# Two-layer decoder trunk: modulation in 512-column tiles, first pair's chunks ahead of the last values, output transposes with a bank of their own

## The chip, the cores and the metric

One NeuronCore of one Trainium2 chip runs the whole program. The metric is the device time of one execution in microseconds (us); lower is better. TensorE is called PE, VectorE DVE, ScalarE ACT, GpSimd POOL and SyncE SP.

## What is computed

A trunk of two decoder layers over 512 tokens of width 1024, in float32, conditioned by a vector c. Each sub-layer is RMSNorm, then a shift and a scale that come from c, then the mixer or the FFN, then RMSNorm, a gate, and the residual add:

```python
def ada_mod(c_act, w, b, n):
    m = c_act @ w + b
    return jnp.split(m[:, None, :], n, axis=-1)
...
        shift, scale, gate = ada_mod(c_act, mod_mix_w[l], mod_mix_b[l], 3)
...
        h = rms_norm(x, norm_pre_mix[l]) * (1.0 + scale) + shift
        if l < N_A_LAYERS:
            y = dilated_mixer(h, a_w_qkv[l], a_w_o[l], cos, sin)
...
        x = x + gate * rms_norm(y, norm_post_mix[l])
```

Layer A's mixer has three groups of 8 heads of 64 (window and dilation 128/1, 512/4, 2048/16), each with its own q, k and v from `a_w_qkv`; the groups' outputs are merged by softmax over their log-denominators. Layer B is differential attention with 8 heads. Both FFNs are gated convolutions of 2816 features. Almost all the arithmetic is the products with the weights.

## The kernel before, in words

**Numbers.** A float32 operand is split into a head `hi` (rounded to the PE's fp32r form, written by ACT) and a rest `lo = full - hi` (DVE), and a product is three PE products: hi·hi, hi·lo, lo·hi. Weights come in chunks of 128 x 1024 by SP's queue into `raw` (three buffers, L404 to L431), are split into `whi` (ACT, L965) and `wlo` (DVE, L1374), and are used by 24 PE products of 512 columns. Chunk n+3 is loaded when chunk n's rest is done.

**Order.** There is no planner: each engine has its own stream, written out by hand, with counting semaphores. `tjob` is a stream of small PE jobs (transposes, one-column products) that share two PSUM banks in turn (`job`, L516): a job waits until the job two before it has been read.

**The start (L652 to L727 on PE, L1079 to L1131 on ACT, L1576 to L1617 on DVE).** SP loads x (2 MB), then eight tiles `mstart` of the first modulation matrix, 1024 rows by 256 columns each, two and then a chunk of value weights in turn (L434). Of a pair of tiles, the shift's 256 columns are made on PE alone (`shift_columns`, L674: 16 one-column products, 32 instructions), the scale's by a chain of eight multiply-adds on DVE (`scale_sums`, L1576) and two column sums over partitions on PE (`scale_columns`, L684). Both Sine operations of the rope tables and the four scalings of x are ACT's (L1085 to L1092). PE turns x in eight jobs of four tiles (L719), ACT copies each to `z0` (L1097). Then, for each of four pairs of feature tiles, ACT writes gain·z + shift twice (full and head, L1107, L1108), DVE the rest (L1611), and PE runs the values chunk of that pair (`values_chunk`, L701). The next pair's shift and scale jobs stand ahead of each values chunk on PE (L722).

**Layer A's attention.** PE then runs the values of groups 1 and 2 (eight chunks), and the six q/k chunks of the first pair of heads (`first_pair`, L750). Each q/k chunk is rotated by DVE (`rope`, L1626, four operations), headed by ACT (L1158) and rested by DVE (L1645, L1647). `attend_pair` (L761) handles a pair of heads in four classes of positions. With `proj` it runs the next pair's six chunks between its own steps. The last turn has none: per pass p it makes the scores of p+1, transposes of the finished output of pair p (`turn_o`, L807, two-bank jobs too; ACT reads the head at L1149, DVE the rest at L1707), transposes of the probabilities, and the products with the values (L804). Warming products (`keep_warm`, L508) fill in. DVE finds maxima (L1694) and sums one half of later modulation per mod_half (L1480), four multiply-adds of 256 columns.

**The token stages.** `token_stage` (L607) multiplies the mixer's output with its out matrix and adds the gated norm. It waits until the last output is transposed and read, runs the first chunk's two token tiles (12 products), spreads the gains over the partitions (`spread_gain`, L542, from diagonals made by DVE at L1387), waits until ACT has read them (L977), and goes on.

Of the kernel before, what the change touches and what calls it, by code (L numbers as in the profile page):

```python
# [114 lines left out]
def yoco_trunk(nc, x, c, positions, mod_mix_w, mod_mix_b, mod_ffn_w, mod_ffn_b,  # L115
# [16 lines left out]
    WARM = 24  # L132
# [10 lines left out]
    with ExitStack() as ctx:  # L143
# [174 lines left out]
        qk_rests = signal("qk_rests", "gsplit")  # L318
        table_natural = signal("table_natural", "table_natural")
# [49 lines left out]
        x_scaled = signal("x_scaled", "x_scaled")  # L369
        m_known = signal("m_known", "m_known")  # L370
# [8 lines left out]
        V_HALVES = (0, 0, 1, 1, 1, 1, 1, 2, 1, 1, 1, 2)  # L379
# [21 lines left out]
        def _(sp):  # L401
# [32 lines left out]
            for n in range(DT // 2):  # L434
                for j in (n, n + DT // 2):
                    sp.dma_start(mstart[:, j], columns(mod_mix_w[0], 2 * P * j, 2 * P)).then_inc(mods_landed[j].sems[0], 16)
                load_values(0, n)
# [3 lines left out]
            for pair in range(PAIRS):  # L441
                for g, w in KINDS:
                    load(columns(a_w_qkv[0][:, (g * 3 + w) * A_INNER:(g * 3 + w + 1) * A_INNER], pair * P))
# [35 lines left out]
        def _(pe):  # L479
# [127 lines left out]
            def token_stage(hi, lo, kt, diags=None, gated=False, norms=True):  # L607
# [6 lines left out]
                pe.wait_ge(*at.done(t_free, -2))  # L614
                pe.wait_ge(*at.done(t_free, -1))
                for b in range(3):
                    pe.wait_ge(*at.done(acc_free, -1 - b))
                for k in range(kt - 3):
                    operands(k)
                    for t in range(NT):  # L620
                        if k == 0 and t == 2 and diags is not None:

                            for diag in diags:
                                spread_gain(diag)
                            pe.wait_ge(*at.done(t_free, -2))
                            pe.wait_ge(*at.done(t_free, -1))
# [47 lines left out]
            def shift_columns(j):  # L674

                bank = job()
                pe.wait_ge(*at.done(mods_landed[j]))
                for half in range(2):
                    for k in range(DT):
                        ins = pe.matmul(bank[:, half:half + 1], mstart[:, j, k, tile_cols(half)], csil[:, k:k + 1],  # L680
                                        start=(k == 0), stop=(k == DT - 1))
                job_done(ins)

            def scale_columns(j):  # L684

                pe.wait_ge(*at.done(m0_summed, j))
                columns_of([macc0[:, 2 * j + half, :] for half in range(2)])

            def values_chunk(g, c):
# [5 lines left out]
                for t in range(NT):  # L695
                    if g and c == 0:
                        pe.wait_ge(*at.done(v_out, t - NT))
                    for k in (2 * c, 2 * c + 1):
# [22 lines left out]
            scale_columns(0)  # L721
            for c in range(DT // 2):  # L722
                if c < DT // 2 - 1:
                    shift_columns(c + 1)
                    scale_columns(c + 1)
                values_chunk(0, c)
            at.passed("h", DT)  # L727
            for g in (1, 2):
                for c in range(DT // 2):
                    values_chunk(g, c)  # L730
                    if (g, c) in ((1, 2), (2, 2)):
                        pair_columns(2 * g - 2, 2)
# [17 lines left out]
            def first_pair():  # L750

                for s in range(6):
# [4 lines left out]
                    if s == 1:  # L757
                        pair_columns(4, 2)
                pe.wait_ge(*at.done(v_out, -1))

            def attend_pair(proj, pair):  # L761
# [45 lines left out]
                def turn_o(n):  # L807

                    turn_tiles([oA[:, n, t, :] for t in range(NT)])
# [40 lines left out]
                if not proj:  # L850
                    keep_warm(2, ps[:, 0, :])
                    pe.wait_ge(*at.done(o_out, -1))
                    turn_o(PAIRS - 1)

            first_pair()
# [1211 lines left out]
```

## Time and profile before

| | us |
|---|---|
| median of 3 runs | 1525.46 |
| lowest, highest | 1522.84, 1529.31 |
| the profiled execution | 1524.3 |
| its span | 1522.5 |
| mean granted PE clock | 0.963 |

The span is that of one profiled execution; the 1.8 us beside it lie around the program. The page splits the span into 40 slices of 38.06 us, and gives for each the busy share of an engine in tenths and the PE clock that was granted, in tenths of full speed (0.5 is 1.2 GHz). DMA moves 313 GB/s in the first slice and 113 on average.

### The profile page before, as it was taken

To read this page: it belongs to the slowest core of one execution; us is meant where nothing else is said; L and a number is where in the kernel's file an instruction comes from. 1 tells how busy PE (TensorE), PEld (TensorE's weight loads), DVE (VectorE), ACT (ScalarE), POOL (GpSimd) and SP (SyncE) were. 2 spreads that over 40 slices of the span, in tenths; PEclk is the share of its full clock that TensorE was granted. 3 is DMA by queue.
4 is the path that set the end of the run, shared out by engine and by line. 5 is a ranking of instruction groups with operands and counts; after the bars stand their busy time and mean duration, and the time that the engine had idled before them with its cause. 6 is when DMAs were issued, how large, how long until landed. Compare 5 with 4: busy or idle time off the path is not lost.

```text
span 1522.5 us, 18985 instructions
## 1 busy us (share of the span) xinstructions
PE 1444.0 (95%) x7234; PEld 1188.0 (78%) x7243; DVE 886.9 (58%) x1540; ACT 584.0 (38%) x1003; POOL 136.5 (9%) x218
## 2 busy tenths in 40 slices
PE   6999899997899999999999999888799999999998
PEld 5888788886788878887887877676579888887886
DVE  5557687684168777763556675766256644443223
ACT  6333343443353334332115454455243333333112
POOL 1010001000021111110113000010021000000000
PEclk9799999896999999999999999999799999999999
DMA  9364334230026655553652212111015433333231
GB/s 313 124 195 145 95 109 126 83 111 14 15 77 200 199 174 178 182 179 97 199 174 61 61 56 59 55 55 56 28 56 153 138 97 97 97 97 90 91 96 69
DMA packets 176787, 171.40 MB, mean 113 GB/s; under 512 B 5205, under 2 KB 153030, under 8 KB 176710
## 3 DMA queue, kind: packets, MB, share of 16 engines
q1 hardware_dynamic: 162352, 119.59, 26.2%
q0 software_dynamic: 13824, 50.34, 10.2%
q8 instruction: 52, 0.85, 0.2%
q10 hardware_dynamic: 534, 0.41, 0.1%
q14 instruction: 25, 0.20, 0.0%
HBM read 168.22 MB, written 2.10 MB: 112 GB/s over the span
## 4 chain that ended last, share of the span: by engine, by line
PE 80%; issue 12%; DVE 5%; POOL 1%; ACT 1%; DMA 0%; SPq 0%; POOLq 0%; ACTq 0%; DVEq 0%
PE ps L553 21%; PE ps L485 14%; PE ps L487 14%; PE ps L486 14%; PE ps L701 5%; PE ps L804 3%; PE ps L770 2%; PE ps L528 2%; PE ps L680 1%; PE ps L539 1%; PE ps L603 1%; POOL small L2027 1%; PE ps L547 0%; PE ps L937 0%; DVE hlo L1442 0%
## 5 line engine op out<-in xcount | busy, mean ns | idle before, releaser
L1374 DVE TENSOR_TENSOR wlo<-raw,whi 128x1024 fp32r<-128x1024 f32 x204 | 249.0, 1222 | 285.5 <-ACT whi L965 285.4
L485 PE MATMUL ps<-hhi,whi 128*128 128x512 f32 (+1 forms) x1016 | 395.7, 390 | 3.5 <-DVE hlo L1442 3.5
L487 PE MATMUL ps<-hhi,wlo 128*128 128x512 f32 (+1 forms) x1016 | 387.5, 381 | 0.0
L486 PE MATMUL ps<-hlo,whi 128*128 128x512 f32 (+1 forms) x1016 | 385.6, 380 | 0.0
L965 ACT ACTIVATE whi<-raw 128x1024 fp32r<-128x1024 f32 x204 | 214.1, 1051 | 275.5 <-PE ps L553 197.2
L485 PEld LDWEIGHTS ps<-hhi,whi 128*128 128x128 f32 x1016 | 191.9, 189 | 40.1 <-issue 5.4
L487 PEld LDWEIGHTS ps<-hhi,wlo 128*128 128x128 f32 x1016 | 191.5, 188 | 38.1
L486 PEld LDWEIGHTS ps<-hlo,whi 128*128 128x128 f32 x1016 | 191.9, 189 | 36.5 <-issue 1.0
L1492 DVE SCALAR_TENSOR_TENSOR macc<-mraw,csil,macc 128x256 f32<-128x256 f32 x294 | 142.2, 484 | 10.1 <-DMA mraw<-in_mod_ffn_w_dram 0.9
L553 PE MATMUL ps<-whi,ghi 128*128 128x512 f32 x352 | 110.7, 395 | 2.0 <-issue 2.0
L553 PE MATMUL ps<-wlo,ghi 128*128 128x512 f32 x352 | 110.4, 394 | 0.0
L553 PE MATMUL ps<-whi,glo 128*128 128x512 f32 x352 | 110.4, 394 | 0.0
L1785 DVE SCALAR_TENSOR_TENSOR tmp<-ps,convc,tmp 128x511 f32<-128x511 f32 x88 | 65.8, 748 | 47.5 <-ACT tmp L1256 44.8
L1266 ACT ACTIVATE ghi<-tmp 128x512 fp32r<-128x512 f32 x44 | 27.8, 632 | 150.0 <-DVE tmp L1801 150.0
L553 PEld LDWEIGHTS ps<-whi,ghi 128*128 128x128 f32 x352 | 65.5, 187 | 19.0 <-issue 3.2
L553 PEld LDWEIGHTS ps<-wlo,ghi 128*128 128x128 f32 x352 | 65.9, 187 | 16.3
L553 PEld LDWEIGHTS ps<-whi,glo 128*128 128x128 f32 x352 | 65.8, 187 | 16.2
L1256 ACT ACTIVATE tmp<-ps,convc 128x512 f32<-128x512 f32 x44 | 34.1, 776 | 107.0 <-PE ps L487 107.0
L1983 POOL DMA_DIRECT2D mraw<-in_mod_ffn_w_dram x48 | 36.3, 756 | 370.5 <-DVE macc L1492 293.4
L485 PE MATMUL ps<-khi,whi 128*128 128x512 f32 (+1 forms) x144 | 57.7, 401 | 4.4 <-DVE klo L1442 4.4
L1801 DVE TENSOR_TENSOR tmp<-ps,tmp 128x512 f32<-128x512 f32 x44 | 30.3, 690 | 53.1 <-issue 42.4
L1311 ACT ACTIVATE prob<-ps,nmax 128x128 f32<-128x128 f32 (+3 forms) x64 | 33.2, 523 | 67.2 <-DVE nmax L1866 67.2
(223 smaller groups left out, 2039.5 us busy)
## 6 DMA issues: line engine op xcount, KB each, us to landing
mraw<-in_mod_ffn_w_dram POOLq DMA_DIRECT2D x48, 512.0 KB, 4.0
raw<-in_ffn_w_gate_dram SPq DMA_DIRECT2D x44, 512.0 KB, 3.8
raw<-in_ffn_w_up_dram SPq DMA_DIRECT2D x44, 512.0 KB, 3.8
raw<-in_ffn_w_down_dram SPq DMA_DIRECT2D x44, 512.0 KB, 3.6
raw<-in_a_w_qkv_dram SPq DMA_DIRECT2D x36, 512.0 KB, 3.7
mraw<-in_mod_mix_w_dram POOLq DMA_DIRECT2D x32, 512.0 KB, 3.9
mstart<-in_mod_mix_w_dram SPq DMA_DIRECT2D x8, 1024.0 KB, 12.3
mraw<-in_kv_mod_w_dram POOLq DMA_DIRECT2D x16, 512.0 KB, 3.9
```

Of the source, the lines that this page charges most:

```text
L485: pe.matmul(out_, whi[:, slot, cols], rhs_hi, start=first, stop=False)
L486: pe.matmul(out_, whi[:, slot, cols], rhs_lo, start=False, stop=False)
L487: return pe.matmul(out_, wlo[:, slot, cols], rhs_hi, start=False, stop=last)
L553: mm = pe.matmul(ps[:, 2 * t + half, :], part[:, k, tile_cols(t)], w[:, slot, half * 512:half * 512 + 512], start=(first and w is whi and ...
L701: mm = pe.matmul(ps[:, t, :], a[:, k, tile_cols(t)], b[:, slot, w], start=(k == 0 and n == 0), stop=(k == DT - 1 and n == 2))
L804: mm = pe.matmul(pv_acc[:, cols], probT[:, hh, tile_cols(e)], v, start=(e == 0), stop=(e == 5))
L965: act.activation(whi[:, slot, :], raw[:, slot, :], ACT.Copy).then_inc(*at.here(hi_ready, ahead))
L1256: act.activation(tmp[:, 0, :], acc[at.at("bank", 3)], ACT.Identity, bias=convc[:, base + 3 * FT + ft:base + 3 * FT + ft + 1], scale=convc[ ...
L1374: dve.tensor_tensor(wlo[:, slot, :], raw[:, slot, :], head, ALU.subtract).then_inc(*at.here(lo_ready, ahead))
L1492: ins = dve.scalar_tensor_tensor(sum_, src, factor, sum_, ALU.mult, ALU.add)
L1785: ins = dve.scalar_tensor_tensor(conv, bank[:, 0:T - shift], tap(t, ft), conv, ALU.mult, ALU.add)
L1983: pool.dma_start(mraw[:, at.at("mod", 2)], src).then_inc(*at.here(m_landed))
```

## The change

1. The modulation matrix's tiles are 512 rows by 512 columns, four for the first half of the features (shift and scale), then two value chunks, then four for the second half. Of each half, one tile (shift, first 512 rows) is PE's (16 one-column products as before, but for four columns), the other three are DVE's: one chain of four multiply-adds of 512 columns, one of eight. PE sums eight columns over the partitions (`start_sums`).
2. Two of the four scalings of x are DVE's. The eight transposed tiles use four banks. The Sine operations come later on ACT. The last four tiles' full value is DVE's instead of ACT's.
3. PE runs the second sums between the second and third token tile of the second chunk, and eight warming products ahead of the third.
4. The first pair's six q/k chunks, and their loads, come ahead of the values of groups 1 and 2. The column jobs and modulation halves are dealt out anew.
5. In the last turn the finished outputs' transposes have PSUM bank 1 and signals of their own; the order of scores, outputs and warming products is changed.
6. In both mixers' token stages the first 12 (A) or 24 (B) products come ahead of the last output's transposes and of the gain spreads.

```diff
-            mstart = sb("mstart", [P, DT, DT, 2 * P], F32, start_mem)
+            mstart = sb("mstart", [P, DT, DT // 2, 4 * P], F32, start_mem)
...
-        V_HALVES = (0, 0, 1, 1, 1, 1, 1, 2, 1, 1, 1, 2)
+        V_HALVES = (0, 0, 1, 1, 1, 1, 2, 2, 1, 1, 2, 0)
...
+            for half in range(2):
+                for j in range(4 * half, 4 * half + 4):
+                    col, k0 = half * 4 * P + (D if j % 4 > 1 else 0), j % 2 * (D // 2)
+                    sp.dma_start(mstart[:, j], mod_mix_w[0][k0:k0 + D // 2, col:col + 4 * P].rearrange("(k p) n -> p k n", p=P)).then_inc(mods_landed[j].sems[0], 16)
+                for n in (2 * half, 2 * half + 1):
+                    load_values(0, n)
...
+            load_pair(0)
             for g in (1, 2):
                 for n in range(DT // 2):
                     load_values(g, n)
+            for pair in range(1, PAIRS):
+                load_pair(pair)
```

PE, the token stage, the start, and the last turn:

```diff
+                def spreads():
+
+                    if turn_last is not None:
+                        turn_last()
+                    for diag in diags or ():
+                        spread_gain(diag)
+                    pe.wait_ge(*at.done(t_free, -2))
+                    pe.wait_ge(*at.done(t_free, -1))
+
                 for b in range(3):
                     pe.wait_ge(*at.done(acc_free, -1 - b))
+                for k in range(lead):
+                    operands(k, k)
+                    for t in (0, 1):
+                        token_products(hi, lo, (at.n["chunk"] + k) % 3, t, k, k == 0, False)
+                spreads()
...
+            def start_sums(half):
+
+                pe.wait_ge(*at.done(m0_summed, 2 * half + 1))
+                columns_of([macc0[:, n, :] for n in range(8)])
...
             shift_columns(0)
-            pe.wait_ge(*at.done(x_scaled, NT - 1))
+            pe.wait_ge(*at.done(x_scaled, 1))
+            pe.wait_ge(*at.done(x_scaled_too, 1))
             for k in range(DT):
-                turn_tiles([xn0[:, t, tile_cols(k)] for t in range(NT)])
...
+                if k < 4:
+                    pe.wait_ge(*at.done(t_free, -1 - k % 2))
+                else:
+                    pe.wait_ge(*at.done(z_out, k - 4))
+                for t in range(NT):
+                    ins = pe.transpose(ps[:, 4 + k % 4, tile_cols(t)], xn0[:, t, tile_cols(k)], identf[:])
+                ins.then_inc(*at.here(xn_turned, k))
+            pe.wait_ge(*at.done(z_out, DT - 1))
+            start_sums(0)
+            shift_columns(4)
+            values_chunk(0, 0)
+            values_chunk(0, 1, lambda: start_sums(1))
+            keep_warm(WARM_START, ps[:, 4, :])
+            values_chunk(0, 2)
+            values_chunk(0, 3)
...
                 def turn_o(n):
 
-                    turn_tiles([oA[:, n, t, :] for t in range(NT)])
+                    pe.wait_ge(*at.done(o_split, -1))
+                    for t in range(NT):
+                        ins = pe.transpose(ps[:, 1, tile_cols(t)], oA[:, n, t, :], identf[:])
+                    ins.then_inc(*at.here(o_turned))
+                    at.passed("ojob")
...
                     scores_pair(0)
+                    turn_o(0)
+                    scores_pair(1)
                     for p in range(CLASSES):
-                        if p < CLASSES - 1:
-                            scores_pair(p + 1)
-                            turn_o(p)
-                        else:
-                            pair_columns(14, 2)
-                        keep_warm(2, ps[:, 0, :])
+                        keep_warm(1, ps[:, 0, :])
                         turn_prob(p, 0)
                         if p:
-                            values(p - 1, 1, -4 if p < 3 else -5)
-                        keep_warm(2, ps[:, 0, :])
+                            values(p - 1, 1, -5 if p == 3 else -4)
+                        else:
+                            keep_warm(2, ps[:, 0, :])
                         turn_prob(p, 1)
+                        if p < CLASSES - 2:
+                            scores_pair(p + 2)
                         values(p, 0, -4)
+                        if p < CLASSES - 2:
+                            turn_o(p + 1)
+                        elif p == CLASSES - 2:
+                            pair_columns(14, 2)
...
             first_pair()
+            for g in (1, 2):
+                for c in range(DT // 2):
+                    values_chunk(g, c)
+                    if (g, c) in ((1, 2), (2, 1), (2, 3)):
+                        pair_columns({(1, 2): 0, (2, 1): 2, (2, 3): 4}[g, c], 2)
+            pe.wait_ge(*at.done(v_out, -1))
```

DVE, the start and the last turn:

```diff
+            start_chain((1,), 0, 0)
+            shift_read(0)
+            start_chain((2, 3), 4, 1)
             split_rest(0)
...
+            sums_read(0)
+            h_rest(0, True)
+            h_rest(1, True)
+            split_rest(1)
+            start_chain((5,), 0, 2)
+            h_rest(2, True)
+            h_rest(3, True)
+            shift_read(1)
+            start_chain((6, 7), 4, 3)
+            split_rest(2)
+            sums_read(1)
+            for k in range(4, DT):
+                h_rest(k, False)
...
                     maxima(0)
+                    maxima(1)
                     for p in range(CLASSES):
-                        if p < CLASSES - 1:
-                            maxima(p + 1)
                         inverses(p)
                         if p < 2:
                             mod_halves(1)
+                        at.passed("tjob", 4)
+                        if p < CLASSES - 2:
+                            maxima(p + 2)
                         if p < CLASSES - 1:
-                            rest_of_o(p)
-                        else:
+                            rest_of_o(p, ps[:, 1, :]).then_inc(*at.here(o_split))
+                            at.passed("ojob")
+                        if p == CLASSES - 2:
                             pair_columns(14, 2)
```

## Rows read from the trace of the kernel before

**Rows 1.** The page: busy time by engine, then the granted clock in 40 slices.
```profile
PE 1444.0 (95%) x7234; PEld 1188.0 (78%) x7243; DVE 886.9 (58%) x1540; ACT 584.0 (38%) x1003; POOL 136.5 (9%) x218
...
PEclk9799999896999999999999999999799999999999
```

**Rows 2.** The chain of waits, 0 to 460 us: start, us, engine, tile, line.
```profile
17.94 6.96 PE ps L680 x32
...
32.41 5.57 PE ps L680 x32
...
38.83 8.22 PE ps L701 x24
47.05 3.46 PE ps L680 x32
...
62.75 30.61 PE ps L701 x120
...
94.15 22.50 PE ps L701 x96
...
171.80 0.66 PE ps L528 x6
...
222.31 1.92 PE ps L770 x13
...
229.93 0.66 PE ps L528 x6
...
278.11 1.78 PE ps L539 x16
```

**Rows 3.** Four-us stretch: us, then PE, PEld, DVE, ACT, POOL; granted clock; DMA.
```profile
36.00:40.00 4.00, 4.00 (x17) 3.81 (x17) 3.88 (x10) 1.29 (x2) 0.00 (x0) 0.50 1.08 350
```

**Rows 4.** The page's costliest groups: busy, mean ns of one, idle before.
```profile
L1374 DVE TENSOR_TENSOR wlo<-raw,whi 128x1024 fp32r<-128x1024 f32 x204 | 249.0, 1222 | 285.5 <-ACT whi L965 285.4
...
L965 ACT ACTIVATE whi<-raw 128x1024 fp32r<-128x1024 f32 x204 | 214.1, 1051 | 275.5 <-PE ps L553 197.2
...
L1492 DVE SCALAR_TENSOR_TENSOR macc<-mraw,csil,macc 128x256 f32<-128x256 f32 x294 | 142.2, 484 | 10.1 <-DMA mraw<-in_mod_ffn_w_dram 0.9
```

**Rows 5.** Instructions in order of time, the start: start, us, what, idle before.
```profile
12.10 2.15 DVE L1557 SCALAR_TENSOR_TENSOR ang<-ang 128x512 f32<-128x512 f32 x3
...
30.42 1.94 ACT L1097 ACTIVATE z<-ps 128x512 f32<-128x512 f32 x3 [0.26 <-PE ps L528]
...
42.17 1.75 POOL L1983 DMA_DIRECT2D mraw<-in_mod_ffn_w_dram  x2 [23.10 <-DMA mstart<-in_mod_mix_w_dram]
```

**Rows 6.** The same view, between the first pair's chunks and its scores.
```profile
157.88 0.72 DVE L1633 STREAM_SHUFFLE tmp<-ps 128x512 f32<-128x512 f32 x1
...
161.94 0.76 PE L770 MATMUL ps<-khi,qhi 64*128 64x512 f32 x3 [4.71 <-DVE qlo L1647]
```

**Rows 7.** The same view, the last turn and the stage behind it.
```profile
343.97 0.49 PE L770 MATMUL ps<-khi,qhi 64*128 64x512 f32 x3
...
353.10 1.10 ACT L1149 ACTIVATE ohi<-ps 128x512 fp32r<-128x512 f32 x1 [3.30 <-PE ps L528]
...
355.77 1.04 DVE L1707 TENSOR_TENSOR olo<-ps,ohi 128x512 fp32r<-128x512 f32 x1
356.86 0.21 PEld L528 LDWEIGHTS ps<-identf,prob 128*128 128x128 f32 x2 [2.50 <-DVE olo L1707]
...
381.00 0.20 PEld L528 LDWEIGHTS ps<-identf,prob 128*128 128x128 f32 x2 [1.80 <-DVE olo L1707]
...
394.55 0.31 ACT L1190 ACTIVATE oA<-ps,rden 128x64 f32<-128x64 f32 x1 [1.76 <-PE ps L804]
...
398.11 0.30 PEld L553 LDWEIGHTS ps<-whi,ohi 128*128 128x128 f32 x2 [2.78 <-issue]
...
405.19 0.30 PEld L553 LDWEIGHTS ps<-whi,ohi 128*128 128x128 f32 x2 [1.58 <-ACT gb L977]
```

**Rows 8.** The same view, layer B's last transposes.
```profile
1078.80 0.72 PEld L528 LDWEIGHTS ps<-identf,osb 128*128 128x128 f32 x4 [2.33 <-DVE osb L1895]
```

More of the change, by code:

```diff
@@ L432, in load_values, with load_pair @@
                 at.passed("chunk")
[L434 to L437, printed above, removed]
+            for half in range(2):
[4 more added lines that the diff above has]
+                    load_values(0, n)
+            def load_pair(pair):
+                for g, w in KINDS:
+                    load(columns(a_w_qkv[0][:, (g * 3 + w) * A_INNER:(g * 3 + w + 1) * A_INNER], pair * P))
+            load_pair(0)
             for g in (1, 2):
@@ L677, in shift_columns, with values_chunk @@
                 pe.wait_ge(*at.done(mods_landed[j]))
[L678 to L681, printed above, removed]
+                for n in range(4):
+                    for k in range(DT // 2):
+                        ins = pe.matmul(bank[:, n:n + 1], mstart[:, j, k, tile_cols(n)], csil[:, k:k + 1],
+                                        start=(k == 0), stop=(k == DT // 2 - 1))
                 job_done(ins)
[L684 to L689, printed above, removed]
+            def start_sums(half):
+                pe.wait_ge(*at.done(m0_summed, 2 * half + 1))
+                columns_of([macc0[:, n, :] for n in range(8)])
+            def values_chunk(g, c, between=None):
                 pe.wait_ge(*at.done(lo_ready))
@@ L695, in values_chunk @@
                 for t in range(NT):
+                    if t == 2 and between is not None:
+                        between()
                     if g and c == 0:
                         pe.wait_ge(*at.done(v_out, t - NT))
+                        if g == 1 and t < 2:
+                            pe.wait_ge(*at.done(pair_free, t - 2))
                     for k in (2 * c, 2 * c + 1):
@@ L1245, in _ @@
             first_pair()
+            for g in (1, 2):
+                for c in range(DT // 2):
+                    values_chunk(g, c)
+            at.passed("tjob", 3)
             for pair in range(PAIRS):
@@ new lines, in _, with start_chain @@
+            dve.wait_ge(*at.done(x_scale))
+            for t in (2, 3):
+                dve.tensor_scalar(xn0[:, t, :], x_tok[:, t, :], X_RMS[:, t:t + 1], None, ALU.mult).then_inc(*at.here(x_scaled_too))
+                at.passed("x_scaled_too")
+            def start_chain(tiles, dst, number):
+                sum_ = macc0[:, dst:dst + 4, :].rearrange("p a n -> p (a n)")
+                for n, j in enumerate(tiles):
+                    dve.wait_ge(*at.done(mods_landed[j]))
+                    for k in range(DT // 2):
+                        src, row = mstart[:, j, k, :], j % 2 * (DT // 2) + k
+                        if n == 0 and k == 0:
+                            ins = dve.tensor_scalar(sum_, src, csil[:, row:row + 1], None, ALU.mult)
+                        else:
+                            ins = dve.scalar_tensor_tensor(sum_, src, csil[:, row:row + 1], sum_, ALU.mult, ALU.add)
+                        if n < len(tiles) - 1 or k < DT // 2 - 1:
+                            chain(ins)
+                ins.then_inc(*at.here(m0_summed, number))
@@ new lines, in shift_read, with sums_read @@
+            def shift_read(half):
+                bank = job_ready()
+                col = MIX[0] + 4 * half
+                job_read(dve.tensor_tensor(modc[:, col:col + 4], bank[:, 0:4], bcol[:, col:col + 4], ALU.add))
+            def sums_read(half):
+                bank = job_ready()
+                col, gain = MIX[0] + 4 * half, MIX[0] + DT + 4 * half
+                dve.wait_ge(*at.done(t_free, -1))
+                dve.tensor_tensor(modc[:, col:col + 4], modc[:, col:col + 4], bank[:, 0:4], ALU.add)
+                job_read(dve.tensor_tensor(modc[:, gain:gain + 4], bank[:, 4:8], bcol[:, gain:gain + 4], ALU.add))
+                dve.wait_ge(*at.done(t_free, -1))
+                dve.scalar_tensor_tensor(presc[:, 4 * half:4 * half + 4], modc[:, gain:gain + 4], 1.0,
+                                         vcol[:, PRE_MIX + 4 * half:PRE_MIX + 4 * half + 4], ALU.add, ALU.mult).then_inc(*at.here(m_known, half))
@@ new lines, in h_rest @@
+            def h_rest(k, whole):
+                if not whole:
+                    gain, shift = presc[:, k:k + 1], modc[:, MIX[0] + k:MIX[0] + k + 1]
+                    dve.wait_ge(*at.done(m_known, 1))
+                    dve.wait_ge(*at.done(h_ready, k - 3))
+                    chain(dve.tensor_scalar(tmp[:, k % 3, :], z0[:, k, :], gain, shift, ALU.mult, ALU.add))
+                dve.wait_ge(*at.done(h_hi, k))
+                dve.tensor_tensor(hlo[:, k, :], tmp[:, k % 3, :], hhi[:, k, :].bitcast(F32), ALU.subtract).then_inc(*at.here(h_ready, k))
@@ L1617, in _ @@
+            at.passed("chunk")
+            split_rest()
             at.passed("h", DT)
@@ L1671, in rest_of_chunk, with values_chunk @@
                 split_rest()
-            for step in range(1, 3 * DT // 2):
+            def values_chunk(step):
                 rest_of_chunk()
                 mod_halves(V_HALVES[step])
-                if step == 8:
-                    pair_columns(0, 2)
-            pair_columns(2, 2)
+                if step in (7, 10):
+                    pair_columns(0 if step == 7 else 2, 2)
+            for step in range(1, 4):
+                values_chunk(step)
             def first_pair():
@@ L1756, in attend_pair @@
                 if not proj:
-                    rest_of_o(PAIRS - 1)
+                    job_read(rest_of_o(PAIRS - 1, job_ready()))
             first_pair()
+            for step in range(4, 12):
+                values_chunk(step)
+            pair_columns(4, 2)
             for pair in range(PAIRS):
```

159 lines of the change are left out of this document (50 added, 109 removed).

## The prediction

> **What bounds the kernel now.** The page first: TensorE (PE) is busy for 1444 us, 95% of the span [rows 1], so the time falls only where PE waits, where it works at the lower clock, or where work leaves it. The clock row has a 7 in its second slice (38 to 76 us) and a 6 in its tenth (343 to 381); these are stages that the change touches. The chain of waits [rows 2] then gives the order. Up to 38.8 us PE runs one-column products and transposes; from there to 93.4 us it runs the values, 168 products; from 161.9 us it attends. The one-column products (32 instructions) take 6.96 us at the start and 3.46 at 47.05, twice the pace: the same work at the two clock levels, 1.2 and 2.4 GHz. The 24 products after 38.83 take 8.22 us, against 96 in 22.50 later (0.234 each, 5.6 for 24).
>
> **The start.** x is scaled half on ScalarE (ACT), half on VectorE (DVE), but the first one-column block ends at 24.9 as before [rows 2], and DVE must still read it (0.2): transposes from 25.2. They use four banks, so PE does not wait for copies, but ACT's eight copies of about 0.65 each [rows 5] and one split of 1.05 between them [rows 4] end them at 32.9, a little later than now (32.4). DVE's own chains: a 512-wide multiply-add costs 0.72 (2.15 for three [rows 5]), so 4 operations 2.8 us and 8 operations 5.8; behind its two scalings of x the first ends at about 23.4; the second starts when the first shift columns are read (25.1) and ends at 31.0, under the transposes. PE's first sums (8 columns, 16 instructions) take between 1.8 (all at the upper clock, as at 278.11 [rows 2]) and 3.5 us; I take 2.2, since the second block's 5.57 for 32 says the clock is still up for its first third. PE ends them at 35.1. Then comes the one shift block of the second half, 6.95 us at the lower clock: 42.1. DVE's four small reads and ACT's first pair of modulated tiles end by 39.5, so PE sets the start of the values, 42.1 instead of 38.8: **3.3 us lost**.
>
> From there PE now needs 93.4 - 38.8 = 54.5 us for 168 products. After the change: 168 x 0.234 = 39.3, the low-clock ramp 8.22 - 5.6 = 2.6, the second sums in the middle of the second chunk 1.8, and eight warming products 1.9: 45.6 us, end 87.7. **Net 5.7 us gained.** DVE's third and fourth chains end at 51.5, the sums are asked for at 52.9; the last four tiles (two DVE operations of some 1.2 us in sum each) are ready at 57 to 61 and chunks three and four ask for them at 59.4 and 65. DVE's cover there is 1.4 us; if it is gone, PE waits so much. The modulation matrix comes in eight loads of 1 MB as before, now four ahead of the first two value chunks; the last landed at about 42 [rows 5], and its reader is now due at 48. POOL's first fetch waits for that load, as before; its sums are due at 60 and later. The two Sine operations on ACT move behind two splits, where ACT has no due work until 50.
>
> The clock is the open price. [Rows 3] show PE busy for 4.00 of 4.00 us and a granted clock of 0.50, after one-column products; so these don't hold it up. The Trainium skill ("TensorE: Matmul & The Clock Gate", Why this matters for your kernels) holds that the clock drops when PE is idle and rises when it is busy. By that rule the second shift block would run at the upper clock and the ramp be gone; the row speaks against it here. From [rows 2] that would be 3.5 + 2.6 = 6.1 us more gained. Against me: if the second sums drop the clock, another ramp of 2.6 is paid.
>
> **First pair ahead of the last values.** Now PE stops 4.71 us behind rope, split and rest of the sixth chunk [rows 6], then needs 9.86 us from the scores to the first transposed probabilities; the next pair, entered at full clock, needs 229.93 - 222.31 = 7.62 [rows 2]. After the change eight value chunks (5.6 us each) lie between, and cover rope and rests. Gone: 4.71 + 2.24 = 6.95. New waits: the second token tile of the next value chunk needs the rope's bank, freed by the shuffle 1.4 us after PE left it (158.60 [rows 6]), just what the first tile takes (six products): 0. The last column job is now behind the last value chunk, and the two modulation halves that it reads are summed in the step before: from the end of the chunk before, split 1.05 + 1.22 [rows 4], gaps 0.4, eight multiply-adds at 0.51 (0.484 [rows 4] and a gap) 4.1, in sum 6.85, against 5.6 for PE's chunk: 1.25 us of wait. It covers ACT's last copy of the values (0.9). DVE's load per first-pair chunk (rope, split, rest) is what those 4.71 us hold, under PE's 5.6. SP issues the loads in the order of use, as before, three buffers deep; the first pair's chunks are as large (512 KB) as the value chunks that they pass. **Gain 5.7 us**; 3.5 if the clock falls at that wait.
>
> **Last turn.** Three times a pass stops because the second transpose bank is read only after DVE's rest of the output: waits of 2.50 down to 1.80 [rows 7]; 6.8 in all. Outputs now have a bank of their own. Warming products fall from 18 to 8: 10 x 0.21 = 2.1 at the upper, 4.3 at the lower clock; I take 3.2. New: before turning output n+1 PE waits until output n is split, and that begins only after this pass's values: normalising 0.31, head 1.10, rest 1.04 [rows 7], three hand-overs 0.5, so 3.0 us, twice (outputs 1 and 2): 6.0. Behind that wait on PE stand the next pass's transposes, and behind these ACT's reads: nothing fills it. The first output's transposes fill 0.7 of the wait for the first maxima. DVE's modulation half leaves the path. 6.8 + 3.2 + 0.7 - 6.0 = **4.7 us gained**. An all-upper clock would make this turn shorter by far, an all-lower one longer; I have worked the order of work through with rows' durations at both: 37 and 59 us, against about 50 now (343.97 to 394.4).
>
> **The two openings of token stages.** Now from the last normalised output (394.86) to the resumed products it is 10.3 us [rows 7]: 3.25 to turn and split, 12 products, gain spreads and their reads. After: 12 products come first (2.8 us at the upper, 5.1 at the lower clock), but the turn, the split and the two diagonals (0.65 for the first, half of a split's 1.22 [rows 4]) then stand bare: 3.9 us, and the spreads and reads 2.5. That is 9.2 to 11.5, and the bare 3.9 us may cost a clock ramp: 0, between -2.5 and +1.6. In layer B 24 products fill the 2.33 us that PE waits for the last normalisation [rows 8], with the same bare stretch behind: 0, between -1.5 and +1.
>
> **Sum.** 5.7 + 5.7 + 4.7 + 0 + 0 = 16.1 us, from the profiled execution's 1524.3 (1.8 more than its span) to 1508.2. The median shown is 1.2 higher: 1509.4. All else (both FFNs, pairs 2 and 3, layer B's heads) keeps its code and its time.
>
> **Rivals.**
> A, the last turn runs mostly at the upper clock: less idle, denser scores. For it: its second half does so already (a 9 follows the 6 [rows 1]). Against: two bare waits of 3 us. 37 to 40 instead of 46 us, 7 us more: 1502. Chance 0.17.
> B, one-column work does not cool the clock: 6.1 us more, 1503. The rule named above says so, [rows 3] says no: 0.05.
> C, the start gives little: a ramp after the second sums, DVE's cover gone (both 2.6 and 1.5), and the lower clock in the first scores (2.2): 16.1 - 6.3 = 9.8 us, 1515.6. For it: the clock fell at 282 us after 16 one-column instructions. Chance 0.18.
> D, slower: the waits for the split output keep PE at the lower clock through the whole last turn (59 instead of 50, in place of 4.7 gained: 13 us) and the bare stretches cost a ramp each (up to 4). It decides if passes 2 to 4 stay at half clock. 16.1 - 17.1 = -1: 1526; beyond 1533 only if C's losses come on top. Chance 0.05.
> E, the parts are made but a wait is where I saw none (the lead's bank, the four-bank transposes), leaving under half: 1518 to 1524, chance 0.07.
> My own case has 0.48.
>
> **How the numbers follow.** The forecast is 1509.4. The bounds of the unknown prices (-2.5 to +1.6, -1.5 to +1, 2.6 for a ramp) give 1504 to 1515 for it alone; to leave out no more than 2 in 10 the range takes in most of A and C: 1499 to 1518. About 0.5% (7.6 us) is what a measurement can tell from no change. Faster by more: my case, A, B, most of C and a little of E, 0.87; within: 0.10; slower: 0.03.
>
> **What would show it.** Right: first value product at 41 to 43 us; three clock ramps in the start become one; no wait for DVE's rope before the first scores, which start at about 153; there a column job that waits some 1 us for the sums; in the last turn two PE waits of about 3 us for DVE's split output and none for a transpose bank; a PE gap of 3 to 4 us behind the 12 leading products. Wrong: one-column products at 0.11 us from 35 us on (B); a granted clock near 1.0 in the whole last turn (A) or near 0.5 (D); the first chunks at 0.43 us per product again after the second sums (C); value chunks that wait for modulation.

## The result and the profile after

| | before | after |
|---|---|---|
| median, us | 1525.3 (4 runs) | 1509.88 (4 runs) |
| lowest, highest | 1522.84, 1529.31 | 1508.62, 1512.3 |
| the profiled execution, its span | 1524.3, 1522.5 | 1512.3, 1510.5 |
| mean granted PE clock | 0.963 | 0.965 |

The ratio is 0.9909, 95% interval 0.9892 to 0.9926: 0.9% faster, 0.0091 x 1525.3 = 13.9 us. The medians of the table differ by 15.4 us. The spans of the profiled executions differ by 12.0, since the changed kernel's profiled execution was the slowest of its four. Here and below, ratios and ranges are of executions in the fast state; two were slow (4044.77 and 1614.13 us, both of the late turns with the waits put back).

The page of the changed kernel, which answers to [rows 1]:

```profile
PE 1438.1 (95%) x7191; PEld 1184.0 (78%) x7191; DVE 892.1 (59%) x1534; ACT 578.3 (38%) x997; POOL 136.7 (9%) x218
...
PEclk9899999985899999999999999999999999999999
```

The second slice rose from 7 to 8, as the start's clock ramps are fewer. The tenth, the last turn, fell from 6 to 5, with an 8 on either side: in this execution that stage got slower. The chain of waits (start, us, engine, tile, line), which answers to [rows 2]:

```profile
17.48 6.97 PE ps L699 x32
24.79 3.66 PE ps L749 x16
...
32.01 1.95 PE ps L551 x16
33.96 5.52 PE ps L699 x32
39.48 11.29 PE ps L724 x36
50.77 1.68 PE ps L551 x16
52.45 2.90 PE ps L724 x12
55.35 1.74 PE ps L523 x8
57.09 11.19 PE ps L724 x48
...
150.11 2.31 PE ps L794 x13
```

The values start at 39.48 (38.83 before), and behind the second sums (50.77) twelve products take 2.90 us, 0.24 each: no ramp. The 96 products of group 0 end at 68.28. The next 72 are now products of the first pair's chunks, of the same size; at 0.234 they end at 85.1, against 93.4 for the 168th product before: 8.2 us. The first scores stand at 150.11 instead of 161.94.

The same chain, closer, ahead of those scores:

```profile
142.71 1.07 ACT whi L1007
143.80 1.23 DVE wlo L1418
145.03 0.28 DVE macc L1532
...
148.52 0.50 DVE macc L1536
149.06 1.05 PE ps L551 x8
...
159.21 0.66 PE ps L540 x6
```

The wait for rope and rest of [rows 6] is gone. In its place the last column job waits for DVE's eight multiply-adds, as predicted, but for 0.8 us only. From the scores to the first transposed probabilities it is 9.10 us (9.86 before).

The last turn in the same view:

```profile
332.78 3.21 PE ps L794 x13
...
384.57 2.49 PE ps L828 x12
387.07 4.35 PE ps L565 x12
395.10 2.00 PE ps L559 x4
397.86 18.43 PE ps L565 x78
```

It takes 332.78 to 387.07, 54.3 us (50.5 before), and then 10.8 to the resumed products, as before. What PE waits for in that stretch (us in total, times, longest):

```profile
PE ps L835 <- DVE olo L1776: 5.0, 2, 2.5
PE ps L559 <- DVE tmp L1431: 3.2, 1, 3.2
PE ps L794 <- DVE nmax L1764: 1.0, 1, 1.0
```

The two predicted waits for the split output are there, at 2.5 us each, and the predicted bare stretch (3.2) behind the twelve leading products. The windows of that turn (stretch; us, then PE, PEld, which is PE's loading of weights, DVE, ACT, POOL; granted clock; DMA share, GB/s):

```profile
340.00:350.00 10.00, 8.88 (x54) 7.28 (x53) 5.53 (x14) 4.59 (x10) 0.00 (x0) 0.71 0.00 0
350.00:360.00 10.00, 8.61 (x48) 7.92 (x48) 3.05 (x8) 4.13 (x10) 0.00 (x0) 0.64 0.01 2
360.00:370.00 10.00, 7.49 (x34) 7.04 (x35) 2.99 (x7) 3.05 (x6) 0.00 (x0) 0.50 0.00 0
370.00:380.00 10.00, 10.00 (x50) 9.69 (x50) 1.29 (x4) 4.24 (x9) 0.00 (x0) 0.50 0.00 0
380.00:390.00 10.00, 10.00 (x40) 8.74 (x40) 0.00 (x0) 1.81 (x5) 0.00 (x0) 0.50 0.01 2
```

PE is at its lower level, 1.2 GHz, from about 353 us to the end of the turn. Layer B's opening, in the chain again:

```profile
1065.29 2.04 PE ps L976 x8
1067.33 6.64 PE ps L565 x24
...
1076.97 2.00 PE ps L559 x4
```

**Where the 12.0 us lie**, cut at these rows and those of before (layer B's last products of that kind stood at 1074.73):

| | predicted | profiled executions |
|---|---|---|
| start, to the 168th product | 5.7 | 8.2 |
| from there to the first transposed probabilities | 5.7 | 4.4 |
| on to the last turn | 0 | -1.4 |
| last turn | 4.7 | -3.9 |
| opening A, and layers to 1065.29 | 0 | 2.1 |
| from 1065.29 to the end, opening B in it | 0 | 2.6 |

### The profile page after: what moved, and what is told of

It reads as the page before. It is cut to its first block, busy times and chain, and to the rows that moved or that the text cites. A ratio compares the mean times of both kernels' runs of the same rounds, so it can differ in the third digit from the quotient of the medians.

```text
span 1510.5 us, 18878 instructions
## 1 busy us (share of the span) xinstructions
PE 1438.1 (95%) x7191; PEld 1184.0 (78%) x7191; DVE 892.1 (59%) x1534; ACT 578.3 (38%) x997; POOL 136.7 (9%) x218
## 3 DMA queue, kind: packets, MB, share of 16 engines
q0 software_dynamic: 13824, 50.34, 10.3%
## 4 chain that ended last, share of the span: by engine, by line
PE 80%; issue 12%; DVE 4%; ACT 2%; POOL 1%; DMA 0%; SPq 0%; POOLq 0%; ACTq 0%; DVEq 0%
PE ps L565 21%; PE ps L497 14%; PE ps L499 14%; PE ps L498 14%; PE ps L724 4%; PE ps L828 3%; PE ps L794 2%; PE ps L540 2%; PE ps L551 1%; PE ps L615 1%; POOL small L2101 1%; PE ps L699 1%; PE ps L559 1%; DVE macc L1536 0%; PE ps L523 0%
```

## The experiments

All ratios are to the kernel before, on the same chip, in five rounds (the second profile of the waits put back in one).

### The changed kernel again

> The changed kernel once more, as the control of this group. Theory (mine): its gain is 5.7 + 5.7 + 4.7 us in prediction, but in the first trace it came as some 8 us in the start, 4.6 in the middle, 4.6 in layer B, and the last turn was 3.8 us longer (54.3 instead of 50.5 us) because the PE clock was low for nearly all of it. If that is bound to the code, this run's last turn is low again (over 45 us of low clock between its first scores and the token stage) and takes 53 to 55 us; total 0.990 to 0.992 of before. Rival (chance of the clock): the low stretches fall elsewhere, and the turn takes anything from 40 to 55 us.

1509.44 us, 0.9905 (0.9883 to 0.9927): as before. But its profiled execution had another last turn, in the chain of waits:

```profile
334.43 2.71 PE ps L794 x13
...
381.16 3.70 PE ps L565 x12
```

46.7 us, what was predicted (46), with a clock of 0.73 to 0.83 in the windows from 340 to 370 us, in the same order of work. The theory above, 53 to 55 us each time, did not hold. One and the same program differs by 7.6 us in this stage, with a mean granted clock of 0.56 in the one turn and 0.73 in the other.

### The last turn's order undone

```diff
                     scores_pair(0)
-                    turn_o(0)
-                    scores_pair(1)
                     for p in range(CLASSES):
-                        keep_warm(1, ps[:, 0, :])
+                        if p < CLASSES - 1:
+                            scores_pair(p + 1)
+                            turn_o(p)
+                        else:
+                            pair_columns(14, 2)
+                        keep_warm(2, ps[:, 0, :])
                         turn_prob(p, 0)
...
```

(and the rest of the turn's order, ACT's and DVE's order, and the shared banks, as before).

> The changed kernel with the last turn's order, warming products and transpose banks as before (its last output still turned behind the 12 leading products). Theory (the new order is shorter at equal clock, but with fewer warming products the clock stays low): here the turn takes about 50 us with two or three stretches at the upper clock, so this is 3 to 4 us faster than the changed kernel. Rival (the order itself gains, and chance of the clock took it): the turn takes 50 to 60 us, same or slower than the changed kernel. Prediction's own term: it would be 4.7 us slower.

1508.12 us, 0.9904 (0.9886 to 0.9922): equal to the control on the same chip. Profiled, the turn took 48.9 us, from the first row of the chain to the second:

```profile
330.53 2.85 PE ps L794 x13
...
379.46 2.85 PE ps L565 x12
```

So the new order of the last turn, as it was made, is worth nothing that five rounds can tell (the intervals are 0.2% wide on either side): neither the 3 to 4 us of the theory nor the 4.7 of the prediction shows. The gain is made elsewhere. In this turn PE waits three times for the split output, 5.9 us in all, and its mean granted clock is 0.72.

### More warming products in the last turn

```diff
-                        keep_warm(1, ps[:, 0, :])
+                        keep_warm(4, ps[:, 0, :])
                         turn_prob(p, 0)
                         if p:
                             values(p - 1, 1, -5 if p == 3 else -4)
-                        else:
-                            keep_warm(2, ps[:, 0, :])
+                        keep_warm(4, ps[:, 0, :])
                         turn_prob(p, 1)
```

> The changed kernel with four warming products ahead of each of the eight groups of probability transposes (32 instead of 6, and the 2 at the end kept). Theory (the clock is what the new turn lacks): they bring the clock up, the turn takes 40 to 46 us instead of 54, so 8 to 14 us faster than the changed kernel. Rival (the two waits for the split output are what costs; the clock does not follow warming products): 26 more products cost 5.5 us at the upper and 11 us at the lower clock, and the turn takes 58 to 64 us.

1513.42 us, 0.9933 (0.9918 to 0.9949): 0.28% or 4 us more than the control. The turn took 51.1 us with a clock of 0.67, 0.67, 0.82, 0.83 and 1.00 in the windows from 340 us. That lies between the two theories. Over the whole turn the clock is 0.77 against the control's 0.73, and the added products cost more than that gave.

### Each output's transposes behind the next pass's probability transposes

```diff
                         turn_prob(p, 1)
+                        if 0 < p < CLASSES - 1:
+                            turn_o(p)
                         if p < CLASSES - 2:
                             scores_pair(p + 2)
                         values(p, 0, -4)
-                        if p < CLASSES - 2:
-                            turn_o(p + 1)
-                        elif p == CLASSES - 2:
+                        if p == CLASSES - 2:
                             pair_columns(14, 2)
```

> The changed kernel with output n+1 turned behind the next pass's second group of transposes instead of at the end of the pass, so PE need not wait for DVE's split of output n (two waits of 2.5 us, one of 2.2 in the trace). Theory: the two waits go whatever the clock does, turn 49 to 50 us if the clock stays low, 5 us faster than the changed kernel. Rival (the waits are only moved to the next thing that PE needs, ACT's reads of the transposes): under 2 us.

1494.65 us, 0.9826 (0.98 to 0.9852): 0.8% below the control, some 12 us. The chain:

```profile
330.06 2.80 PE ps L794 x13
...
364.90 2.85 PE ps L565 x12
```

34.8 us for the turn. PE's waits in it:

```profile
PE ps L540 <- DVE modc L1522: 1.1, 1, 1.1
PE ps L794 <- DVE nmax L1764: 1.0, 1, 1.0
```

and its windows, columns as above:

```profile
330.00:340.00 10.00, 8.60 (x48) 7.62 (x49) 5.11 (x14) 2.67 (x6) 0.00 (x0) 0.53 0.18 52
340.00:350.00 10.00, 10.00 (x86) 8.59 (x84) 6.82 (x19) 7.95 (x19) 0.00 (x0) 0.95 0.01 2
350.00:360.00 10.00, 8.78 (x75) 8.20 (x76) 4.34 (x11) 7.06 (x15) 0.00 (x0) 1.00 0.00 0
360.00:370.00 10.00, 8.01 (x54) 6.67 (x54) 0.60 (x1) 2.88 (x6) 0.00 (x0) 1.00 0.01 2
```

The waits for the output are gone and the clock is up from 341 us on. The turn is 11.9 us shorter than the control's 46.7, and 5.0 of that are the waits themselves. The other 6.9 are what is left by subtraction; the mean clock of the turn went from 0.73 to 0.85, which can give as much. That the waits hold the clock down isn't shown by this run, since the transposes were moved too.

### The late turns with the waits alone put back

```diff
                         values(p, 0, -4)
+                        if p < CLASSES - 2:
+                            pe.wait_ge(*at.done(o_split, -1))
                         if p == CLASSES - 2:
```

(against the late turns).

> The late turns (each output's transposes behind the next pass's probability transposes), and TensorE's wait for VectorE's split output put back where the changed kernel has it, at the end of the first two passes, with nothing else moved. So the wait is there and the transposes are not. Theory W (a bare wait costs its own 2.5 us twice and, beyond that, keeps the clock at its lower level): the two waits appear, low clock stretches come back in the last turn (over 20 us of it, where the late turns had 14), and the turn takes 43 or more instead of 34.9; ratio 0.988 to 0.992. Theory I (idle time only): the two waits appear, the turn is 34.9 + 5 = 40 us and the low stretches stay at about 14 us; ratio 0.985 to 0.987. Theory T (the transposes' place did it, not the wait): no change against the late turns, 35 to 37 us.

1515.95 us, 0.9944 (0.9924 to 0.9963). The wait list again, its first line:

```profile
PE ps L523 <- DVE olo L1778: 5.0, 2, 2.5
```

The chain and the windows of its profiled execution:

```profile
331.77 2.80 PE ps L794 x13
...
376.46 1.68 PE ps L565 x7
```

```profile
340.00:350.00 10.00, 7.49 (x50) 6.15 (x49) 7.39 (x19) 4.84 (x10) 0.00 (x0) 0.84 0.00 1
350.00:360.00 10.00, 9.10 (x56) 8.39 (x54) 2.90 (x7) 4.68 (x11) 0.00 (x0) 0.69 0.01 2
360.00:370.00 10.00, 7.88 (x54) 7.55 (x54) 1.78 (x4) 6.12 (x13) 0.00 (x0) 0.83 0.00 0
370.00:380.00 10.00, 9.04 (x62) 7.66 (x62) 0.65 (x4) 2.54 (x8) 0.00 (x0) 1.00 0.01 2
```

Nothing was moved here, only PE stopped twice for 2.5 us, and the turn is 44.7 instead of 34.8: 5.0 for the waits, 4.9 for the clock. All profiles of the last turn, from its first scores to the end of its products with the values, one number for each profiled execution:

| | the turn, us | mean granted clock in it |
|---|---|---|
| kernel before | 50.5 | 0.70 |
| changed kernel | 54.3, 46.7 | 0.56, 0.73 |
| last turn as before: order undone, start alone, middle alone | 48.9, 48.9, 45.9 | 0.72, 0.72, 0.81 |
| more warming products | 51.1 | 0.77 |
| late turns, in five profiles | 34.8, 34.8, 34.8, 35.0, 35.0 | 0.85, 0.85, 0.85, 0.85, 0.88 |
| late turns, waits put back, two profiles | 44.7, 44.7 | 0.77, 0.77 |

The five are the run above and the four further runs below that keep the late turns. The spread within either kind is far below the 9.9 us between them. So in this turn the waits themselves pull the clock down, which neither idle time alone nor the place of the transposes would give.

The times say more than the trace, and not all of it is understood. The profiled execution was at 1499.3 us (clock 0.977), 4.5 us above that of the late turns on the same chip. The others of the same kernel stand at 1515.4 to 1517.6 with a mean clock of 0.961 to 0.965; the ratio, 0.9944, is above theory W's 0.988 to 0.992. Beside the late turns on the same chip (0.9792, below) it is 1.5%, 23 us. It is also above the changed kernel's 0.9905, whose turn has the same two waits and is no shorter.

A second profile was taken to see an execution near 1516:

> The late turns with the waits put back, a second profile of the same kernel: its profiled execution was at 1499.3 us, but five of the others at 1515 to 1518, with a mean clock of 0.963 instead of 0.977. If what holds the clock down there is the waits in the last turn (theory W), an execution near 1516 has its extra lower clock in the last turn or directly behind it: the turn then takes 55 us or more, instead of 44.7, and the stretches elsewhere are as before. If the extra low stretches lie spread over the other stages, the waits' price in that turn stays at the 10 us of the first profile, and the rest is of another cause that these runs don't name.

1516.92 us, 0.9949 (0.9927 to 0.9971), but the profiled execution was again the lowest of its runs (1503.69), with the same turn of 44.7 us:

```profile
336.29 2.84 PE ps L794 x13
...
381.00 2.86 PE ps L565 x12
```

The medians of the two measurements lie 17 and 13 us above their profiled executions. Where that time lies stays open: no trace shows it, and only the mean clock of those runs (0.961 to 0.970) points to the clock.

### The start alone, the middle alone

The first takes from the changed kernel the middle, the last turn and the openings (the values of groups 1 and 2 ahead of `first_pair` again, among other lines):

```diff
+            for g in (1, 2):
+                for c in range(DT // 2):
+                    values_chunk(g, c)
+                    if (g, c) in ((1, 2), (2, 2)):
+                        pair_columns(2 * g - 2, 2)
             first_pair()
-            for g in (1, 2):
...
```

> Only the start of the change: middle, last turn and both openings as before. My theory: the gain of the start is that of the prediction plus a clock that holds through half of the shift block; the four value chunks of group 0 end at 68 to 69 us (76.3 before), so 7 to 8 us faster in the trace, 5 to 8 in the times. Rival (the prediction's own term): 5.7 us. Rival (the start gains little, and the rest made it up): under 3 us.

1516.92 us, 0.9949 (0.9933 to 0.9965): 7.8 us, by the interval 5.3 to 10.2, which does not tell the theory from the prediction's 5.7. In its profile the 168th value product ends at 86.75 us, 6.6 before the kernel before, and the values of group 0 begin at 41.29. Its wait for the rest of the sixth chunk is the one of [rows 6], in order of time:

```profile
155.33 0.76 PE L797 MATMUL ps<-khi,qhi 64*128 64x512 f32 x3 [4.71 <-DVE qlo L1708]
```

The second puts the middle alone into the kernel before (the same lines the other way round, the loads, and V_HALVES).

> The kernel before with only the first pair's chunks ahead of the values of groups 1 and 2. The prediction's term: 4.71 us of wait gone, 1.25 us of wait for the modulation sums new, 2.24 us less of low clock in the first scores: 5.7 us faster. Rival (the clock falls all the same): 3.5 us. In the traces so far the first scores to the first transposes took 9.1 us once, so a low clock there; of this run's own trace: scores start 3.5 us earlier; clock high or low decides 7.6 or 9.1 to 9.9 us behind it.

1519.77 us, 0.9973 (0.9962 to 0.9983): 4.1 us, by the interval 2.6 to 5.8. From the scores to the first transposed probabilities it took 10.6 us. No wait for the rest is left, and the sums are waited for instead:

```profile
PE ps L540 <- DVE macc L1493: 0.8, 1, 0.8
```

Start and middle together: 0.9949 x 0.9973 = 0.9922, against 0.9905 for the whole. What is left, 0.0017 or 2.6 us for openings and last turn, lies within the intervals.

### The late turns, with the token stages' openings as before

```diff
                 def spreads():
 
-                    if turn_last is not None:
-                        turn_last()
                     for diag in diags or ():
...
+                if turn_last is not None:
+                    turn_last()
+                    turn_last = None
+                    pe.wait_ge(*at.done(t_free, -2))
+                    pe.wait_ge(*at.done(t_free, -1))
                 for b in range(3):
                     pe.wait_ge(*at.done(acc_free, -1 - b))
```

(against the late turns; layer B without its lead of two, and two warming products ahead of layer A's last output transposes, as before.)

> The kernel with the later output transposes, and both openings of the token stages as before (last output turned and split ahead of the first products, 12 products only in layer B). The prediction's terms say 0 for layer A (-2.5 to +1.6) and 0 for layer B (-1.5 to +1): times as the kernel with later transposes, 1494 to 1497. Rival (the openings are worth what layer B showed in the first trace, 2.4 us, plus as much in A): 3 to 5 us slower than that kernel.

1497.35 us, 0.9809 (0.9785 to 0.9834), against 0.9826 and 0.9792 for the late turns with the new openings, each measured on another chip: no difference that can be measured.

### One modulation half earlier

```diff
-        V_HALVES = (0, 0, 1, 1, 1, 1, 2, 2, 1, 1, 2, 0)
+        V_HALVES = (0, 0, 1, 1, 1, 1, 2, 2, 1, 2, 1, 0)
```

on top of the late turns.

> The kernel with the later output transposes, and one modulation half moved from the step ahead of the last column job to the step ahead of that, so the job's sums are ready in time. Theory: the wait of 0.8 us between the last value chunk and the column job goes, nothing else changes: 0.8 us faster, at most 3 if the clock then holds through the first scores. Rival (the half is late in its new place too): 0.

1490.18 us, 0.9765 (0.9743 to 0.9787). That was lower than the wait for the sums (0.9 us) can explain, so both were run side by side.

> The late turns once more, beside the next kernel on the same chip. If the first measurement of each was fair, its ratio to the kernel before is 0.982 again, within 0.003.

> The late turns with one modulation half moved from the eleventh to the tenth value chunk, beside the late turns. The half's place removes a wait of TensorE of at most 1 us before the first scores, so by that theory the two kernels differ by 1 us or less (ratios within 0.001). The rival is that the clock stays up at the first scores as the gap is gone: 3 to 9 us less (ratio 0.976 to 0.980, as first measured).

The late turns: 1494.76 us, 0.9792 (0.9768 to 0.9816). With the half moved: 1491.05 us, 0.979 (0.9763 to 0.9816). In the first profile with the half moved the wait is

```profile
PE ps L551 <- DVE macc L1536: 0.3, 1, 0.3
```

and in the second there is none; the first scores to the first transposed probabilities take 7.6 us in both, and 7.6 in both profiles of the late turns too. So the half's place is worth its own fraction of a microsecond at most, and the lower first figure was not found again. Both kernels beat the one before and the changed one: about 1491 to 1495 us, 2% below the kernel before.

## Why the prediction was right, and where it was not

The forecast of 1509.4 us came out at 1509.88. That the two are so close is partly luck, since errors cancel: in the profiled execution the last turn was 8.6 us worse than its term, the start 2.5 better, the middle 1.3 worse, and of the stages put at nothing one lost 1.4 us and two gained 4.7.

**Start: 5.7 predicted, 8.2 in the profile, 7.8 when run alone.** What was off here is the one-column block ahead of the values: put at 6.95 us at the lower clock, it took 5.52, since the clock stayed up longer. The transposes were done at 32.0, not 32.9, and the sums took 1.95, not 2.2. Together 2.6 us: the values began at 39.5 instead of 42.1. From there the prediction gave PE 45.6 us for 168 products, and it needed 85.1 - 39.5 = 45.6. One ramp instead of three, and no wait for modulation: both held in this execution. Part of the 2.6 us is chance. Of the twelve profiled executions with this start, five have the block in 5.3 to 5.9 us and the first value product at 39.5 to 39.8 us; in the other seven it took 6.8, as predicted, and the values began at 40.9 to 42.05. In all twelve the 96 products of group 0 ended at 68.0 to 70.3, where the prediction's figures give 70.9, so the term was 0.6 to 2.9 us too small.

**Middle: 5.7 predicted, 4.4 in the profile, 4.1 alone.** The wait of 4.71 went and one for the sums came, as worked out, 0.8 instead of 1.25. But the entry into the scores at full clock did not come: it took 9.10 us, where 7.62 was forecast. The clock fell there, the case for which the text had 3.5. This too differs between executions: of the nine profiled ones that have the changed start, the new middle and the 0.8 us wait, three took 7.6 us, two 9.1 and 9.2, and four 10.6.

**Last turn: 4.7 predicted, -3.9 in the profile, nothing by the runs.** The order of waits was right: three waits for banks gone, two for the split output in their place, 2.5 each (3.0 predicted). The 6.8 us for the three were read from the rows of PEld; PE itself waits 5.9 us for them, in the kernel before as with the order undone. Since the two new waits are 5.0 us instead of 6.0, what the exchange saves in waiting is 0.9 us, where 0.8 was forecast. The step that failed is the price of the two new waits. They were put into the sum as 6.0 us of idle time, and the clock as a separate chance, a rival that "stays at half clock". The waits alone put back show that the two are one term: 5.0 us of waiting bring 4.9 us or more of lower clock. That is as much as the whole gain forecast for the turn. It does not tell the new order from the old one, though: the old order has three such waits and a mean clock of 0.70 to 0.81 over four profiles, and what they cost in clock was not measured. The control's turn of 46.7 against the 54.3 above shows how far one and the same program spreads here, between the forecast of 46 and rival D's 59. D's condition was met in one profiled execution, for this stage only; its ramps elsewhere did not come.

Rival A, most of the turn at the upper clock (37 to 40 us), did not happen; the reason that the text gave against it, the two bare waits, is borne out. Without them the turn takes 34.8 us at a mean clock of 0.85, with only its first scores at the lower one (0.53 from 330 to 340 us).

**Openings: 0 predicted, nothing measured.** In layer A 10.8 us before and after (10.3 was read for before, from the last normalised output). PE waits 3.2 us for the diagonal, inside the 3.9 that were worked out. In layer B the profile shows 2.6 us gained from there to the end, but undoing both openings changes nothing beyond the interval. From the same products to the end the four profiles with the old opening take 446.8 to 447.8 us, nine of the ten with the new one 442.9 to 446.7, and one 449.2. So some 2 us are likely, less than the times can tell.

**The rest: 0 predicted.** 1.4 us lost in pairs 1 to 3 and 2.1 gained in the layers behind are within what these stages differ by from one profiled execution to the next: 170.7 to 173.8 us from the first transposed probabilities to the last turn, 665 to 671 from the resumed products to layer B's opening, over all profiles. No run was made on them. B (one-column work does not cool the clock) did not come: the first 36 value products take 11.29 us, where 36 at 0.234 would take 8.4. Of C, the lower clock in the first scores came, and in this profile the rest did not: the second sums brought no ramp. It was no empty rival: in the profile with more warming products, whose start is the same, PE waited 0.4 us for the second sums and the 12 products behind them took 4.32 us instead of 2.90.

## What to carry to other kernels

A short bare wait of PE amid small products is not priced by its length: here two of 2.5 us cost 10 in the turn, in both profiled executions, and some 20 in the times, of which no trace has located more than those 10. Put what must wait for another engine behind work that is ready, even if the order looks less natural, and look for it first where a slice of the page is below full clock with little idle time. When a profile of one execution decides over a few microseconds in such a stage, take a second one of the same kernel before reading it.

## What the runs showed of the hardware that was not expected

PE was busy for 10.00 of 10.00 us from 370 to 380 and again from 380 to 390, and the granted clock was 0.50 all that time, though most of this was no one-column work (eight sums at 374.20 are) but transposes of 128 columns and products of 64. In the late turns PE was busy for 8.78 and 8.01 of 10.00 us from 350 to 370 with the same kinds of work, and the clock was 1.00. The Trainium skill ("TensorE: Matmul & The Clock Gate", Why this matters for your kernels) has the clock come back once TensorE is kept busy; the first two rows disagree, the second two show it up with less busy time.

More warming products did not help: with 4 ahead of each group of transposes the windows from 340 to 360 us stood at 0.67, where the control had 0.73 and 0.83.

The same program differs between executions, and its clock with it: the late turns with the waits put back ran at 1499.3 and at 1517.6 us with mean clocks of 0.977 and 0.961.
